# A mixture-of-experts stage on one core: expert blocks of 32 rows on four column groups in place of blocks of 64 on two

## The chip, the cores and the metric

The kernel runs on one core of one Trainium2 chip. The metric is device time in microseconds. TensorE, VectorE (DVE in the rows), ScalarE (ACT), GpSimd (POOL) and SyncE (SP) each run their own stream of instructions and meet at semaphores; transfers run on 16 DMA engines, fed by queues of SyncE, ScalarE and GpSimd.

## The reference, cut to what matters

One step of a decoder layer: a projection, sparse attention and a state-space scan side by side, an output projection, then a mixture of experts and a last norm. 2080 tokens (2048 of the prompt, 32 sampled) each go to 2 of 32 experts. The change concerns the experts:

```python
def run(args):
    xb, e = args                       # rows of one expert, (rows, 1024)
    hdn = jax.nn.silu(xb @ w_gate[e]) * (xb @ w_up[e])      # (rows, 512)
    return hdn @ w_down[e]             # (rows, 1024)
...
contrib = (yr.astype(jnp.float32) * row_w[:, None]).astype(xf.dtype)
return jnp.zeros_like(xf).at[row_tok].add(contrib)
```

All data are float32. One expert's weights are 6 MB: gate and up 1024 x 512 each, down 512 x 1024.

## The kernel before

The program is a row of stages. `mix_out` ends by placing the assignments: each expert's rows are padded to whole blocks of `BR` = 64 slots, every assignment gets a slot, and two one-hot tables (`onerow`, `oneblk`), multiplied on TensorE, give `rows`, the token that stands in each slot of each of up to `MAXBLK` blocks. `experts` works through the blocks in order, and `combine` gathers each token's two result rows from `yslot` in HBM by slot and adds them.

In `experts` every engine walks the same blocks (`over_blocks`): `first` for the first block of an expert, and a loop over `rest` for the others. For block b:

- GpSimd copies the block's token numbers to `cur` and issues two indirect gathers of 128 KB, one for each 32 rows, into `xg` (each token row is spread over four partition groups of 32 as quarters of 256 columns). It starts as soon as VectorE has turned the block before.
- VectorE transposes `xg` into `xT` in squares of 32 (`turn_rows`).
- TensorE (`gate_up`) multiplies `xT`, the stationary operand of 64 columns, with the gate and up weights. The 512 hidden columns are two halves, one on each half of the array's columns, so PSUM partitions 0 to 63 hold the first half for the 64 rows and 64 to 127 the second.
- ScalarE takes Silu of the gate half (`gate`), VectorE multiplies with up (`hidden`), TensorE transposes the product (`turn_hidden`), ScalarE copies it out of PSUM as `hT` (`turned_hidden`).
- TensorE (`down`) multiplies `hT` with the down weights, the 1024 output columns again in two halves. It runs one block late: after the gate/up of block b+1, and it waits for `hT` and for the copy of the block before it out of PSUM.
- VectorE copies the result from PSUM to `y` (`rows_done`). There is one `y`, so the copy of block b waits until all stores of block b-1 have landed (semaphore `y_st`):

```python
def rows_done(b):
    v.wait_ge(sm["y_ok"], 2 * b + 2)
    v.wait_ge(sm["y_st"], 32 * b + 32)
    v.tensor_copy(y[:], py[:]).then_inc(sm["y_cp"], 1)
```

- ScalarE stores `y` to `yslot` in two DMAs of 64 rows by 512 columns (`store`), after the Silu of the next block and before its `turned_hidden`.

SyncE loads the weights of experts into two buffers. The gate and up weights of expert e are issued when the last gate/up of expert e-2 is done, its down weights when the last down of e-2 is done.

Of the kernel before, what the change touches and what calls it, by code (L numbers as in the profile page):

```python
# [15 lines left out]
P = 128  # L16
# [26 lines left out]
BR = 64  # L43
MAXBLK = 98
# [2568 lines left out]
def mix_out(nc, io, keep):  # L2613
# [5 lines left out]
    with Alloc(nc, "mo") as a:  # L2619
# [30 lines left out]
        big = a.sb("big", [P, NT * 2, NEXP])  # L2650
# [5 lines left out]
        oneblk = a.sb("oneblk", [P, NT * 2, MAXBLK])  # L2656
# [121 lines left out]
        def _(v):  # L2778
# [129 lines left out]
            for c in range(2):  # L2908
                sl = slice(q * c, q * c + q)
                v.tensor_tensor(onerow[:, sl, :], bc(rowio[:].unsqueeze(1), [P, q, BR]), bc(lowf[:, sl].unsqueeze(2), [P, q, BR]), ALU.is_equal)  # L2910
                for i in range(q * c, q * c + q):
                    r = slice(0, rows_of(i // 2))
                    v.tensor_scalar(oneblk[r, i, :], blkio[r, :], blkf[r, i:i + 1], keep["tok"][r, i // 2:i // 2 + 1], ALU.is_equal, ALU.mult).then_inc(sm["oh_ok"], 1)
            v.memset(keep["rows"][:, :, MAXBLK:MAXBLK + 1], 0)
            v.wait_ge(sm["map_ok"], 1)
            for q in range(4):
                for hh in range(2):
                    v.tensor_scalar(keep["rows"][32 * q:32 * q + 32, hh, 0:MAXBLK], pl[32 * hh:32 * hh + 32, 0:MAXBLK], 4.0, float(q), ALU.mult, ALU.add)
# [3 lines left out]
        def _(pe):  # L2922
# [51 lines left out]
            for i in range(2 * NT):  # L2974
                r = slice(0, rows_of(i // 2))
                pe.wait_ge(sm["oh_ok"], i + 1)
                mm = pe.matmul(pl[0:BR, 0:MAXBLK], onerow[r, i, :], oneblk[r, i, :], start=(i == 0), stop=(i == 2 * NT - 1))
# [4 lines left out]
def experts(nc, io, keep):  # L2982
# [5 lines left out]
    with Alloc(nc, "ex") as a:  # L2988
# [4 lines left out]
        xg = a.sb("xg", [P, 2, D // 4])  # L2993
        xT = a.sb("xT", [P, KD, 2, 32])
        sg = a.sb("sg", [P, DE // 2])
        hid = a.sb("hid", [P, DE // 2])
        hT = a.sb("hT", [P, 2, 2, BR])
# [3 lines left out]
        names = ("xg_in", "xt_ok", "gu_ok", "sg_ok", "hid_ok", "h_t", "h_ok", "y_ok", "y_cp", "y_st", "zero_ok", "tail_st", "go")  # L3001
        sm = {n: a.sem(n) for n in names}
        gu_in, d_in = [keep["ew_gu_in"], a.sem("gu_in")], [keep["ew_d_in"], a.sem("d_in")]
# [39 lines left out]
        def _(pool):  # L3043
            pool.memset(zero[:], 0.0).then_inc(sm["zero_ok"], 1)
            n = pool.value_load(keep["blocks"][0:1, NEXP:NEXP + 1], min_val=1, max_val=MAXBLK)
            with pool.Fori(0, n + 1) as b:
                pool.wait_ge(sm["xt_ok"], b + 1)
                pool.tensor_copy(cur[:], rows[:, :, ds(b, 1)].squeeze(2))  # L3048
                pool.drain()
                for hh in range(2):  # L3050
                    pool.indirect_dma_start(xg[:, hh, :], None, quarters, bass.IndirectOffsetOnAxis(ap=cur[:, hh:hh + 1], axis=0)).then_inc(sm["xg_in"], 16)  # L3051

        @block.scalar
        def _(s):
# [30 lines left out]
            s.wait_ge(sm["y_st"], n * 32 + 32)  # L3085
# [3 lines left out]
        def _(v):  # L3089
            v.sem_inc(sm["y_cp"], 1)  # L3090
            v.sem_inc(sm["xt_ok"], 1)

            def turn_rows(b):
                v.wait_ge(sm["xg_in"], 32 * b + 32)
# [295 lines left out]
```

## Time and profile before

| | us |
|---|---|
| three runs: median (lowest to highest) | 3298.22 (3292.75 to 3299.91) |
| the profiled execution, its own time | 3290.99 |
| its span, first to last instruction | 3289.2 |
| first gate/up matmul of `experts`, from the span's start | 2276.8 |
| last store of `experts` landed | 3185.8 |

The span is what the profile covers; 1.8 us of the execution's own time lie around it. The stage of the experts is 909 us of it. In the rows below, "idle before" is the time for which an engine waited before an instruction, with what ended it. A matmul of float32 appears as two records.

### The profile page before, as it was taken

The numbers are of one execution on the slowest core, as the hardware profiler recorded it, in microseconds if no ns is written. First come the engines' busy times: TensorE is split into PE (matmuls) and PEld (weight loads), VectorE is DVE, ScalarE is ACT, GpSimd is POOL, SyncE is SP. The second block draws the span as 40 slices with busy tenths as digits, with TensorE's granted clock in tenths as the row PEclk, the third lists the DMA queues.
The fourth block names the chain that finished last, engine by engine and source line by source line (L and its number), as shares of the span: only waits on it lengthen the run. The fifth ranks groups of instructions, "written<-read, shape, count | busy, mean of one in ns | idle before, by whom it ended". The sixth has DMA issues, their size and how long they took to land. (4 is left out here: it accounts for less than half of the span.)

```text
span 3289.2 us, 42132 instructions
## 1 busy us (share of the span) xinstructions
PE 2693.6 (82%) x13682; PEld 1292.4 (39%) x13683; DVE 1626.9 (49%) x3741; ACT 1036.5 (32%) x1887; POOL 815.2 (25%) x940
## 2 busy tenths in 40 slices
PE   7998987966965656777895779995999999999960
PEld 3444333333542334554664544442333333333320
DVE  1146577786766688888873334544111111111126
ACT  1123353573234579874663310010000000000002
POOL 1404031123450333323423400001122121221226
PEclk9999998987877878888997889997999999999985
DMA  6010101012341211100006845543887678787758
GB/s 212 30 49 32 56 13 64 10 37 67 106 131 50 60 31 37 37 27 14 17 14 204 242 124 187 182 133 115 302 299 263 228 259 299 277 288 265 259 186 338
DMA packets 242716, 456.02 MB, mean 139 GB/s; under 512 B 41420, under 2 KB 97214, under 8 KB 242574
## 3 DMA queue, kind: packets, MB, share of 16 engines
q1 hardware_dynamic: 199070, 334.50, 29.7%
q0 software_dynamic: 27872, 89.48, 8.8%
q10 hardware_dynamic: 15632, 30.29, 2.4%
q8 instruction: 71, 1.16, 0.2%
q14 instruction: 71, 0.58, 0.1%
HBM read 368.53 MB, written 85.65 MB: 138 GB/s over the span
## 5 line engine op out<-in xcount | busy, mean ns | idle before, releaser
L784 PE MATMUL pj_cm<-pj_xT,pj_w 128*64 128x512 f32 (+1 forms) x1216 | 397.0, 601 | 8.4 <-ACT pj_xst L682 5.8
L3099 DVE TENSOR_TENSOR ex_hid<-ex_sg,ex_pgu 128x256 f32<-128x256 f32 x83 | 34.9, 421 | 586.5 <-ACT ex_sg L3059 586.5
L3128 PE MATMUL ex_pgu<-pre_down_wgu,ex_xT 128*64 128x512 f32 x1312 | 293.1, 599 | 13.3 <-DVE ex_xT L3095 13.3
L3128 PE MATMUL ex_pgu<-ex_wgu,ex_xT 128*64 128x512 f32 x1344 | 297.7, 595 | 0.4 <-issue 0.4
L784 PEld LDWEIGHTS pj_cm<-pj_xT,pj_w 128*64 128x64 f32 (+1 forms) x1216 | 153.8, 164 | 244.0 <-issue 230.7
L2273 PE MATMUL ap_SB<-keep_kT,ap_qs 64*128 64x512 f32 (+3 forms) x640 | 163.0, 615 | 51.7 <-DVE ap_m L2199 42.5
L2285 PE MATMUL ap_TB<-keep_const,ap_L 128*128 128x128 f32 x1088 | 167.8, 296 | 45.3 <-ACT ap_PT L2021 42.5
L2021 ACT ACTIVATE ap_PT<-ap_TB 128x512 f32<-128x512 f32 (+3 forms) x320 | 154.7, 530 | 150.9 <-PE ap_TB L2285 149.8
L2296 PE MATMUL ap_OB<-ap_PT,keep_V 128*64 128x128 f32 x2176 | 156.4, 305 | 46.6 <-ACT ap_PT L2021 46.6
L3051 POOL DMA_INDIRECT ex_xg<-xn,ex_cur x168 | 161.1, 959 | 104.3 <-issue 104.3
L2285 PEld LDWEIGHTS ap_TB<-keep_const,ap_L 128*128 128x128 f32 x1088 | 124.5, 148 | 149.4 <-issue 63.5
L708 ACT ACTIVATE se_U<-se_sc,se_cand 128x512 bf16<-128x512 f32 (+4 forms) x141 | 162.1, 1151 | 62.9 <-DVEq L529 62.8
L3063 ACT ACTIVATE ex_hT<-ex_ph 128x256 f32<-128x256 f32 x83 | 31.9, 384 | 442.5 <-issue 441.5
L508 DVE TENSOR_SCALAR_CACHE_REDUCE se_U<-se_sc,se_cand 128x384 bf16<-128x384 f32 (+7 forms) x162 | 165.0, 1050 | 12.6
L3048 POOL COPY ex_cur<-pre_rows 128x2 int32 x84 | 15.5, 184 | 617.5 <-DVE ex_xT L3095 617.3
L3128 PEld LDWEIGHTS ex_pgu<-pre_down_wgu,ex_xT 128*64 128x64 f32 x1312 | 91.1, 138 | 186.1 <-issue 172.4
L2031 ACT ACTIVATE ap_L<-ap_L,ap_nm 128x128 f32<-128x128 f32 (+15 forms) x128 | 153.0, 1198 | 35.1 <-DVE ap_nm L2204 30.9
L3128 PEld LDWEIGHTS ex_pgu<-ex_wgu,ex_xT 128*64 128x64 f32 x1344 | 92.9, 137 | 175.3 <-issue 175.3
L2296 PEld LDWEIGHTS ap_OB<-ap_PT,keep_V 128*64 128x64 f32 x2176 | 138.7, 155 | 55.9 <-ACT ap_PT L2021 44.0
L3059 ACT ACTIVATE ex_sg<-ex_pgu 128x256 f32<-128x256 f32 x83 | 31.9, 384 | 401.8 <-PE ex_pgu L3128 401.8
L3144 PE MATMUL ex_py<-ex_wd,ex_hT 128*64 128x512 f32 x672 | 151.4, 592 | 2.3 <-ACT ex_hT L3063 2.3
L2082 DVE TENSOR_SCALAR_CACHE_REDUCE ap_marks<-ap_sc,ap_cand 128x1664 bf16<-128x1664 f32 (+1 forms) x72 | 145.8, 2032 | 5.5
(557 smaller groups left out, 4508.2 us busy)
## 6 DMA issues: line engine op xcount, KB each, us to landing
pre_down_wgu<-in_w_gate SPq DMA_DIRECT2D x16, 2048.0 KB, 9.0
pre_down_wgu<-in_w_up SPq DMA_DIRECT2D x16, 2048.0 KB, 14.8
pre_down_wd<-in_w_down SPq DMA_DIRECT2D x16, 2048.0 KB, 9.4
ex_wgu<-in_w_gate SPq DMA_DIRECT2D x16, 2048.0 KB, 9.3
ex_wgu<-in_w_up SPq DMA_DIRECT2D x16, 2048.0 KB, 14.8
ex_wd<-in_w_down SPq DMA_DIRECT2D x16, 2048.0 KB, 9.6
yslot<-ex_y ACTq DMA_DIRECT2D x166, 128.0 KB, 6.5
pj_x<-in_x_prompt SPq DMA_DIRECT2D x16, 512.0 KB, 4.8
```

Of the source, the lines that this page charges most:

```text
L508: v.tensor_scalar(hits[s][:, 0:keys(h, s)], row_of(h, s), cand[:, s:s + 1].bitcast(F32), None, op, ALU.add, accum_out=cnt[:, s:s + 1])
L708: act_e.activation(hits[s][:, 0:keys(h, s)], row_of(h, s), ACT.Sign, bias=cand[:, s:s + 1].bitcast(F32), scale=-1.0, accum_out=cnt[:, s:s ...
L784: mm = pe.matmul(cm[u % 2][cols * n:cols * n + cols, 0:width_], w[:, k, c0:c0 + cols], xT[:, k, 0:width_], start=(k == 0), stop=(k == KD - 1))
L2021: s_.activation(PT[:, e, o:o + w], TB[t % 2][:, 0:w], ACT.Copy).then_inc(pt_ok, 1)
L2031: s_.activation(L[:, u % 2, e, 0:n], L[:, u % 2, e, 0:n], ACT.Exp, bias=nm[:, h:h + 1], accum_out=rs[:, j % 2, h:h + 1]).then_inc(exp_ok, 1)
L2082: v.tensor_scalar(hits[s][:, 0:keys(s)], row_of(s), cand[:, s:s + 1].bitcast(F32), None, op, ALU.add, accum_out=cnt[:, s:s + 1])
L2273: pe.matmul(SB[:, 2 * (use % 2) + e, 0:w], qs[hs, j % 2, c, :], keep["kT"][hs, o:o + w], start=True, stop=True).then_inc(s_ok, 1)
L2285: mm = pe.transpose(TB[t % 2][:, at:at + P], L[:, u % 2, e, o + at:o + at + P], ident)
L2296: mm = pe.matmul(OB[HD * e:HD * e + HD, P * c:P * c + P], keep["V"][:, kb, HD * e:HD * e + HD], PT[:, e, P * kb:P * kb + P], start=(kb == ...
L3051: pool.indirect_dma_start(xg[:, hh, :], None, quarters, bass.IndirectOffsetOnAxis(ap=cur[:, hh:hh + 1], axis=0)).then_inc(sm["xg_in"], 16)
L3128: mm = pe.matmul(pgu[BR * t:BR * t + BR, :], xT[:, k, :, :], wgu[par][:, k, :, 256 * t:256 * t + 256], start=(k == 0), stop=(k == KD - 1))
L3144: mm = pe.matmul(py[BR * t:BR * t + BR, :], hT[:, k % 2, k // 2, :], wd[par][:, k, 512 * t:512 * t + 512], start=(k == 0), stop=(k == 3))
```

## The change

Blocks become 32 rows long (`BR` = 32, up to 161 of them). A block's columns are spread over four column groups of 32: gate/up takes the 512 hidden columns as four quarters of 128 gate and 128 up columns, down the 1024 output columns as four quarters of 256. The hidden product is then 128 partitions by 128 columns and needs one transpose. The rows of a block come with one gather instead of two; `xg` has two halves, and the gather of block b+2 is issued when the rows of block b have been copied to the new buffer `xa`, from which VectorE transposes. The result is stored by four DMAs of 32 rows by 256 columns. In `mix_out` the one-hot tables take the new sizes (`onerow` 32 columns, `oneblk` 161), and `oneblk` shares its space with an earlier buffer.

```diff
-BR = 64
-MAXBLK = 98
+BR = 32
+MAXBLK = 161
...
-        xg = a.sb("xg", [P, 2, D // 4])
-        xT = a.sb("xT", [P, KD, 2, 32])
+        xg = a.sb("xg", [P, 2 * (D // 4)])
+        xa = a.sb("xa", [P, D // 4])
+        xT = a.sb("xT", [P, KD, BR])
...
-        y = a.sb("y", [P, D // 2])
+        y = a.sb("y", [P, D // 4])
...
-                    sp.wait_ge(sm["gu_ok"], lo * 2)
+                    sp.wait_ge(sm["gu_ok"], lo)
                 load_gate_up(sp, io, wgu[e % 2], e, gu_in[e % 2])
                 if e >= 2:
-                    sp.wait_ge(sm["y_ok"], lo * 2)
+                    sp.wait_ge(sm["y_ok"], lo)
...
-            with pool.Fori(0, n + 1) as b:
-                pool.wait_ge(sm["xt_ok"], b + 1)
-                pool.tensor_copy(cur[:], rows[:, :, ds(b, 1)].squeeze(2))
-                pool.drain()
-                for hh in range(2):
-                    pool.indirect_dma_start(xg[:, hh, :], None, quarters, bass.IndirectOffsetOnAxis(ap=cur[:, hh:hh + 1], axis=0)).then_inc(sm["xg_in"], 16)
+            pool.sem_inc(sm["xg_free"], 2)
+            with pool.Fori(0, (n + 3) >> 1) as g:
+                for half in range(2):
+                    pool.wait_ge(sm["xg_free"], 2 * g + half + 1)
+                    pool.tensor_copy(cur[:, half:half + 1], rows[:, ds(2 * g + half, 1)])
+                    pool.drain()
+                    pool.indirect_dma_start(xg[:, D // 4 * half:D // 4 * half + D // 4], None, quarters,
+                                            bass.IndirectOffsetOnAxis(ap=cur[:, half:half + 1], axis=0)).then_inc(xg_in[half], 16)
...
-                for half in range(2):
-                    s.dma_start(io["yslot"][ds(row, BR), 512 * half:512 * half + 512], y[BR * half:BR * half + BR, :]).then_inc(sm["y_st"], 16)
+                for q in range(4):
+                    s.dma_start(io["yslot"][ds(row, BR), 256 * q:256 * q + 256], y[BR * q:BR * q + BR, :]).then_inc(sm["y_st"], 16)
...
-            def turn_rows(b):
-                v.wait_ge(sm["xg_in"], 32 * b + 32)
-                v.transpose(xT[:].rearrange("p k h t -> p h k t"), xg[:].rearrange("p h (k t) -> p h k t", t=32)).then_inc(sm["xt_ok"], 1)
+            def rows_in(b):
+                v.wait_ge(xg_in[0], 16 * ((b + 2) >> 1))
+                v.wait_ge(xg_in[1], 16 * ((b + 1) >> 1))
+                v.tensor_copy(xa[:], xg[:, ds((b & 1) * (D // 4), D // 4)]).then_inc(sm["xg_free"], 1)
+                v.drain()
+
+            def turn_rows():
+                v.transpose(xT[:], xa[:].rearrange("p (k t) -> p k t", t=32)).then_inc(sm["xt_ok"], 1)
+                v.drain()
...
             def rows_done(b):
-                v.wait_ge(sm["y_ok"], 2 * b + 2)
-                v.wait_ge(sm["y_st"], 32 * b + 32)
-                v.tensor_copy(y[:], py[:]).then_inc(sm["y_cp"], 1)
+                v.wait_ge(sm["y_ok"], b + 1)
+                v.wait_ge(sm["y_st"], 64 * b + 64)
+                v.tensor_copy(y[:], py[:, 0:D // 4]).then_inc(sm["y_cp"], 1)
...
             def rest(b, par):
                 hidden(b)
                 rows_done(b - 1)
+                rows_in(b + 2)
...
                 for k in range(KD):
-                    for t in range(2):
-                        mm = pe.matmul(pgu[BR * t:BR * t + BR, :], xT[:, k, :, :],
-                                       wgu[par][:, k, :, 256 * t:256 * t + 256], start=(k == 0), stop=(k == KD - 1))
+                    for t in range(4):
+                        mm = pe.matmul(pgu[BR * t:BR * t + BR, 0:2 * P], xT[:, k, :],
+                                       wgu[par][:, k, :, P * t:P * t + P], start=(k == 0), stop=(k == KD - 1))
...
                 for k in range(4):
-                    for t in range(2):
-                        mm = pe.matmul(py[BR * t:BR * t + BR, :], hT[:, k % 2, k // 2, :],
-                                       wd[par][:, k, 512 * t:512 * t + 512], start=(k == 0), stop=(k == 3))
+                    for t in range(4):
+                        mm = pe.matmul(py[BR * t:BR * t + BR, 0:D // 4], hT[:, k, :],
+                                       wd[par][:, k, 256 * t:256 * t + 256], start=(k == 0), stop=(k == 3))
```

On ScalarE, in the block loop of an expert, the order before was this (`ex_sg` is the Silu, `ex_hT` the turned hidden rows of the same block, and `yslot<-ex_y` the stores of the block before):

```order
L3059 ACTIVATE ex_sg<-ex_pgu 128x256
L3067 REGISTER_ALU
L3069 ISA
L3069 DMA yslot<-ex_y 64x512
L3069 ISA
L3069 DMA yslot<-ex_y 64x512
L3063 ACTIVATE ex_hT<-ex_ph 128x256
```

And with the change:

```order
L3070 ACTIVATE ex_sg<-ex_pgu 128x128
L3080 ISA
L3080 DMA yslot<-ex_y 32x256
L3080 ISA
L3080 DMA yslot<-ex_y 32x256
L3080 ISA
L3080 DMA yslot<-ex_y 32x256
L3080 ISA
L3080 DMA yslot<-ex_y 32x256
L3074 ACTIVATE ex_hT<-ex_ph 128x128
```

Four issues instead of two now stand between the two activations, each for a quarter of the bytes.

On VectorE, in the same loop, the order before was this (the two `ISA` rows ahead of the copy are its waits for the down projection and for the stores of the block before):

```order
L3099 TENSOR_TENSOR ex_hid<-ex_sg,ex_pgu 128x256
L3094 ISA
L3095 STREAM_TRANSPOSE ex_xT<-ex_xg 128x2x8x32
L3103 ISA
L3104 ISA
L3105 COPY ex_y<-ex_py 128x512
```

And with the change:

```order
L3115 TENSOR_TENSOR ex_hid<-ex_sg,ex_pgu 128x128
L3110 STREAM_TRANSPOSE ex_xT<-ex_xa 128x256
L3120 ISA
L3121 COPY ex_y<-ex_py 128x256
L3104 ISA
L3105 ISA
L3106 REGISTER_ALU x2
L3106 ISA
L3106 COPY ex_xa<-ex_xg 128x256
```

The wait for the gather has moved from ahead of the transpose to behind the copy of `y`, and a copy of the gathered rows is new there.

## Rows read from the trace of the kernel before

**Rows 1.** Windows: the expert stage; busy us and records by engine, granted clock, DMA share.

```profile
core 0: us, PE busy (x) PEld busy (x) DVE busy (x) ACT busy (x) POOL busy (x), PEclk, DMA share, GB/s
...
2276.80:3185.80 909.00, 901.06 (x4150) 296.06 (x4150) 144.34 (x249) 63.76 (x166) 174.45 (x249) 1.00 0.76 264
```

**Rows 2.** Timeline of one block: start, duration, engine, line, what, idle before.

```profile
2601.68 0.69 DVE L3105 COPY ex_y<-ex_py 128x512 f32<-128x512 f32 x1 [2.07 <-PE ex_py L3144]
2601.81 7.09 PE L3128 MATMUL ex_pgu<-pre_down_wgu,ex_xT 128*64 128x512 f32 x32
...
2602.55 1.13 ACTq L3069 DMA_DIRECT2D yslot<-ex_y  x2
2603.73 0.38 ACT L3063 ACTIVATE ex_hT<-ex_ph 128x256 f32<-128x256 f32 x1 [5.20 <-issue]
...
2608.73 3.60 PE L3144 MATMUL ex_py<-ex_wd,ex_hT 128*64 128x512 f32 x16
...
2608.97 0.38 ACT L3059 ACTIVATE ex_sg<-ex_pgu 128x256 f32<-128x256 f32 x1 [4.85 <-PE ex_pgu L3128]
...
2609.73 0.70 DVE L3095 STREAM_TRANSPOSE ex_xT<-ex_xg 128x512 f32<-128x512 f32 x1
...
2610.59 0.18 POOL L3048 COPY ex_cur<-pre_rows 128x2 int32 x1 [7.47 <-DVE ex_xT L3095]
...
2611.71 0.97 POOL L3051 DMA_INDIRECT ex_xg<-xn,ex_cur  x1 [0.94 <-issue]
...
2612.26 0.44 PE L3136 MATMUL ex_ph<-keep_const,ex_hid 128*128 128x128 f32 x2
2612.40 0.37 SPq L196 DMA_DIRECT2D ex_wd<-in_w_down  x1
2612.50 0.69 DVE L3105 COPY ex_y<-ex_py 128x512 f32<-128x512 f32 x1 [2.07 <-PE ex_py L3144]
2612.63 1.08 PE L3128 MATMUL ex_pgu<-pre_down_wgu,ex_xT 128*64 128x512 f32 x4
```

**Rows 3.** The page's groups: one hidden product a block, count, busy, mean ns.

```profile
L3099 DVE TENSOR_TENSOR ex_hid<-ex_sg,ex_pgu 128x256 f32<-128x256 f32 x83 | 34.9, 421 | 586.5 <-ACT ex_sg L3059 586.5
```

**Rows 4.** Timeline of SyncE's weight loads beside three blocks.

```profile
2598.15 0.37 SPq L192 DMA_DIRECT2D ex_wgu<-in_w_gate  x1
2598.56 0.58 SPq L192 DMA_DIRECT2D ex_wgu<-in_w_up  x1
...
2630.61 0.37 SPq L192 DMA_DIRECT2D pre_down_wgu<-in_w_gate  x1
```

**Rows 5.** Line 3069, the two stores at 2602.6 us.

```profile
DMA to landing us min/median/max: 6.2/6.3/6.4
```

**Rows 6.** Line 3069, the two stores at 2613.4 us.

```profile
DMA to landing us min/median/max: 7.2/7.5/7.8
```

**Rows 7.** Line 3069, the two stores at 2624.2 us.

```profile
DMA to landing us min/median/max: 2.6/2.8/2.9
```

**Rows 8.** Timeline of TensorE in the sampled attention: a series on four column groups.

```profile
1790.09 1.95 PE L2602 MATMUL as_OB<-as_V,as_PT 128*32 128x128 f32 x64
```

**Rows 9.** The page's DMA issues: count, KB each, median us from issue to landing.

```profile
ex_wgu<-in_w_gate SPq DMA_DIRECT2D x16, 2048.0 KB, 9.3
ex_wgu<-in_w_up SPq DMA_DIRECT2D x16, 2048.0 KB, 14.8
ex_wd<-in_w_down SPq DMA_DIRECT2D x16, 2048.0 KB, 9.6
```

**Rows 10.** Timeline of VectorE around the start of the expert stage.

```profile
2252.62 1.29 DVE L2910 TENSOR_TENSOR mo_onerow<-mo_rowio,mo_lowf 128x1088 f32<-128x1088 f32 x1
2253.83 4.17 DVE L2913 TENSOR_SCALAR mo_oneblk<-mo_blkio,mo_blkf,keep_const 128x98 f32<-128x98 f32 x17
...
2276.08 0.71 DVE L3095 STREAM_TRANSPOSE ex_xT<-ex_xg 128x512 f32<-128x512 f32 x1 [10.20 <-DMA ex_xg<-xn,ex_cur]
```

**Rows 11.** Windows: a stretch with a recurring gap on TensorE.

```profile
990.00:1050.00 60.00, 40.75 (x219) 17.03 (x217) 39.91 (x58) 35.09 (x43) 0.32 (x1) 0.86 0.08 30
```

**Rows 12.** Timeline of TensorE in that stretch: the gap and its period.

```profile
1004.33 2.81 PE L1719 MATMUL ss_X<-ss_sw,ss_shw 128*128 128x512 f32 x4 [2.58 <-ACT ss_sw L1584]
...
1013.95 1.98 PE L1719 MATMUL ss_X<-ss_sw,ss_shw 128*128 128x512 f32 x4 [2.58 <-ACT ss_sw L1584]
```

More of the change, by code:

```diff
@@ L2655, in mix_out, with oneblk @@
         blki, blkf = a.sb("blki", [P, NT * 2], I32), a.sb("blkf", [P, NT * 2])
-        oneblk = a.sb("oneblk", [P, NT * 2, MAXBLK])
+        ownblk = a.sb("ownblk", [P, OWN, MAXBLK])
+        def oneblk(r, i):
+            return ownblk[r, i, :] if i < OWN else spare[r, (i - OWN) * MAXBLK:(i - OWN + 1) * MAXBLK]
         tp = a.ps("tp")
@@ L2976, in _ @@
                 pe.wait_ge(sm["oh_ok"], i + 1)
-                mm = pe.matmul(pl[0:BR, 0:MAXBLK], onerow[r, i, :], oneblk[r, i, :], start=(i == 0), stop=(i == 2 * NT - 1))
+                mm = pe.matmul(pl[0:BR, 0:MAXBLK], onerow[r, i, :], oneblk(r, i), start=(i == 0), stop=(i == 2 * NT - 1))
             mm.then_inc(sm["map_ok"], 1)
@@ L2992, in experts @@
         cur = a.sb("cur", [P, 2], I32)
[L2993 to L2998 removed]
+        xg = a.sb("xg", [P, 2 * (D // 4)])
+        xa = a.sb("xa", [P, D // 4])
+        xT = a.sb("xT", [P, KD, BR])
+        sg = a.sb("sg", [P, P])
+        hid = a.sb("hid", [P, P])
+        hT = a.sb("hT", [P, 4, BR])
+        y = a.sb("y", [P, D // 4])
         zero = a.sb("zero", [BR, D])
         pgu, ph, py = a.ps("pgu"), a.ps("ph"), a.ps("py")
[L3001 removed]
+        names = ("xg_free", "xt_ok", "gu_ok", "sg_ok", "hid_ok", "h_t", "h_ok", "y_ok", "y_cp", "y_st", "zero_ok", "tail_st", "go")
         sm = {n: a.sem(n) for n in names}
+        xg_in = [a.sem(f"xg_in{i}") for i in range(2)]
         gu_in, d_in = [keep["ew_gu_in"], a.sem("gu_in")], [keep["ew_d_in"], a.sem("d_in")]
@@ L3114, in rest @@
                 rows_done(b - 1)
-            turn_rows(0)
+                rows_in(b + 2)
+            v.wait_ge(xg_in[0], 16)
+            v.tensor_copy(xa[:], xg[:, 0:D // 4]).then_inc(sm["xg_free"], 1)
+            v.drain()
+            turn_rows()
+            v.wait_ge(xg_in[1], 16)
+            v.tensor_copy(xa[:], xg[:, D // 4:D // 2]).then_inc(sm["xg_free"], 1)
+            v.drain()
             over_blocks(v, first, rest)
@@ L3124, in gate_up @@
             def gate_up(b, par):
-                pe.wait_ge(sm["xt_ok"], b + 2)
+                pe.wait_ge(sm["xt_ok"], b + 1)
                 for k in range(KD):
-                    for t in range(2):
-                        mm = pe.matmul(pgu[BR * t:BR * t + BR, :], xT[:, k, :, :],
-                                       wgu[par][:, k, :, 256 * t:256 * t + 256], start=(k == 0), stop=(k == KD - 1))
-                        if k == KD - 1:
-                            mm.then_inc(sm["gu_ok"], 1)
+                    for t in range(4):
+                        mm = pe.matmul(pgu[BR * t:BR * t + BR, 0:2 * P], xT[:, k, :],
+                                       wgu[par][:, k, :, P * t:P * t + P], start=(k == 0), stop=(k == KD - 1))
+                mm.then_inc(sm["gu_ok"], 1)
             def turn_hidden(b):
                 pe.wait_ge(sm["hid_ok"], b + 1)
-                for k in range(2):
-                    mm = pe.transpose(ph[:, k * P:(k + 1) * P], hid[:, k * P:(k + 1) * P], ident)
-                mm.then_inc(sm["h_t"], 1)
+                pe.transpose(ph[:, 0:P], hid[:], ident).then_inc(sm["h_t"], 1)
             def down(b, par):
@@ L3354, in trunk_step @@
         with Alloc(nc, "pre") as b:
-            keep["rows"] = b.sb("rows", [P, 2, MAXBLK + 1], I32)
+            keep["rows"] = b.sb("rows", [P, MAXBLK + 3], I32)
             keep["wo"], keep["wo_in"] = b.sb("wo", [P, KD, D]), b.sem("wo_in")
```

35 lines of the change are left out of this document (18 added, 17 removed).

## The prediction

> **What bounds the kernel now.** I began with the windows of the expert stage. From the first gate/up matmul (2276.8 us) to the landing of the last store (3185.8 us) TensorE is busy 901 of 909 us, its granted clock is 1.00, and the DMA engines are busy 0.76 of the time [rows 1]. So in this stage TensorE is the limit and everything else has room. The timeline of one block then shows the rhythm [rows 2]: gate/up starts at 2601.81 and again at 2612.63, so a block of 64 rows costs 10.82 us. Gate/up takes 6.92 us to the start of the down projection, down 3.53 us to the two transposes of the hidden rows, these 0.37 us. The page counts 83 blocks [rows 3]: 83 x 10.82 = 898 us.
>
> In the same timeline the reader should see a loop that does not touch TensorE. VectorE copies the finished rows out of PSUM into the one buffer `y` (0.69 us), 0.18 us later ScalarE issues two stores (1.13 us), and the next copy into `y` waits until both have landed. How long landing takes depends on what SyncE has in flight. The store at 2602.6 has the next expert's gate and up weights (issued 2598.15) beside it and lands after 6.2 and 6.4 us; the one at 2613.4 has the down weights beside it: 7.2 and 7.8 us; the one at 2624.2 has none: 2.6 and 2.9 us [rows 4 to 7]. The second of two stores is issued 0.64 us after the first (1.13 less its own 0.49). At its worst the loop is 0.69 + 0.18 + 0.64 + 7.8 = 9.3 us. That is under 10.82, so today it costs nothing: VectorE's copy is always released by TensorE [rows 2].
>
> **The change, part by part.**
>
> *Padding and TensorE.* Counting the routing of the reference's inputs gives 4160 row assignments, 81 to 174 an expert: 83 blocks of 64, as the page has it, and 147 of 32. Each 32-row block streams half the columns (256 for 512) through four column groups instead of two. If a group of four costs what a pair does per column, gate/up and down take (6.92 + 3.53) / 2 = 5.23 us. That four groups of 32 do run side by side is shown elsewhere in the trace: 64 matmul records of 128 columns in 1.95 us, 0.122 us a group of four [rows 8]; at 256 columns and 24 groups that bounds the block from above at 24 x 0.244 = 5.86 us (the series' start and end are in it). I take 5.23, because the matmuls of the experts are the same stream. One transpose instead of two: 0.2 to 0.37, taken as 0.30. Block: 5.53 us. 147 x 5.53 = 813 us, **85 us less** (between 85 less and 7 more at 5.86 + 0.30).
>
> *VectorE, ScalarE and the gather.* A 256-column operation with PSUM input takes 0.42 us where 512 columns take 0.69 [rows 2, 3]. VectorE has per block: hidden product, transpose, copy of `y`, and the new copy of the gathered rows, each at most 0.42: under 1.7 of 5.53 us. ScalarE's two activations shrink from 0.38 each. POOL needs 2.1 us from its release to the end of an indirect DMA's issue (2610.59 to 2612.68 [rows 2]), and now has one a block and two blocks, 11 us, for it to land. The stage's first pair of gathers, beside weights and with POOL's start-up, is in after 10.2 us of VectorE's waiting [rows 10], so one gather has more time than two took there; I cost this edit at nothing. If that cover failed, VectorE would wait in the row copy, and the next hidden product behind it.
>
> *Four stores instead of two, and one `y`.* This is the part that decides. ScalarE issues four in 3 x 0.64 + 0.49 = 2.4 us, ahead of the copy of the turned hidden rows, for which the next down projection waits. Without any wait for landings that chain is: end of down to copy 0.17 (2612.33 to 2612.50), copy 0.42, 0.18, issues 2.4, turned hidden rows some 0.38 (between half and all of today's 0.38, with 0.05 of signalling on each side), down 1.8 us (half of 3.60): 5.3 us, just under 5.53. So the issues are hidden, barely. The landing is not. The copy of block b still waits for all stores of b-1, and the loop is 0.42 + 0.18 + 0.05 + L, where L runs from the first issue to the last landing. It exceeds 5.53 when L is over 4.88 us. With no weights in flight the last of four is issued 1.92 us after the first and takes 2.6 to 2.9: L = 4.8 at most; the loop stays hidden. With weights in flight there are three bounds from [rows 5, 6]: the whole set lands with the first store, 6.2 (gate/up) and 7.2 (down); as the present pair, 0.64 + 6.4 = 7.0 and 8.4; each small store needs the whole latency from its own issue, 1.92 + 6.4 = 8.3 and 9.7. In the present pair the second needs as long from its own issue as the first, so I take a value between the second and third bounds, **7.7 and 9.0 us**. The block then lasts 8.35 us beside gate/up and 9.65 beside down.
>
> How long are weights in flight? Gate and up are issued 0.41 us apart and land 14.8 us after the second issue: 15.2 us [rows 4, 9]. Down, issued before that end, follows with half their bytes: 7 us (today 8.6, since it is issued only 1 us before the others land). Per load 15.2 / 8.35 + 7 / 9.65 = 2.55 blocks take 22.2 us in place of 14.1: 8.1 us more. Loads for experts 2 to 31 run beside blocks: 30 x 8.1 = **243 us more**. Queued behind VectorE's wait are its row copy, which frees the gather buffer, and the next hidden product; ScalarE's stores and turned hidden rows wait for the copy, and TensorE's next down projection for those.
>
> *Placement tables.* The one-hot rows go from 98 to 161 columns, 34 of them at 0.245 us [rows 10], at most 0.16 us more each, and the other table halves (two of 1.29). Between 1 us less and 5 more; taken as 0. The zero fill of unused slots runs behind the last weights on SyncE, ahead of the stage's end.
>
> Sum: -85 + 243 = +158 us. The profiled execution took 3290.99 us (span 3289.2), so 3449; it lies 7 us under the median of the three runs shown, so I say **3450**. With the lowest L (6.2, 7.2) the blocks last 6.85 and 7.85 us, a load costs 5.0 us extra, and the sum is +65: 3356. With the highest it is 9.1 us, +187: 3478.
>
> **Where a page disagrees.** No row shows a 32 KB store; the 128 KB stores range from 2.6 us alone to 7.8 beside weights [rows 5 to 7]. The Trainium skill, page "DMA: Bandwidth & Descriptors", section "Anatomy of one DMA", gives a fitted 2.0 us plus bytes at 436 GB/s for a DMA (fitted for those GpSimd issues), so 2.1 us for 32 KB; by it L would be 4.0 us, the loop would stay hidden, and the sum would be -85. The trace agrees with it only where no weights move. The same page's rules for kernel authors advise against many transfers under 64 KB.
>
> **The rivals.**
> - *The stores land in time; TensorE sets the pace; faster.* Small stores of half the bytes might slip between weight packets. It decides if L is under 4.88 us beside weights. For it: 2.6 to 2.9 us alone, half the bytes, and a longer period leaves the DMA engines idler. Against: over half of the present latency beside weights is not there without them (6.4 to 7.8 against 2.9), and that part need not shrink with the bytes. 3291 - 85 = 3206 us, with the median's offset 3210. Chance 0.15. The rule of the Trainium skill's page "DMA: Bandwidth & Descriptors" named above would end here.
> - *The clock falls too.* Beside weights TensorE now has one gap of 2.8 to 4 us a block. Gaps of 2.58 us every 9.6 us stand earlier in the trace, and there the mean granted clock is 0.86 of full speed, switching between 2.4 and 1.2 GHz [rows 11, 12]. Inside a waiting block slower matmuls fit into the gap; but if after each load half of a gate/up (1.7 us) still runs at the lower level, that costs 1.7 us a load: +51 us, 3500. Chance 0.12.
> - *The column groups don't overlap.* Then 24 groups cost twice as much, 10.76 us a block: 147 x 10.76 - 898 = +684, 3975. [Rows 8] speak against it. Chance 0.02.
> - *Gain and loss cancel* (L near 5.7, 2.8 us a load): chance 0.05.
>
> **How the numbers follow.** My case has 0.66 with its own range of 3356 to 3500. The likeliest is 3450; the range of 3300 to 3540 leaves out the faster rival and the last one. Faster 0.15, same 0.05, slower 0.80; 0.2% (6.6 us) is about what a measurement of this kernel can tell.
>
> **What would show it.** Right: VectorE's copy of `y` waits for the DMA of `y` to the slots in 2 to 3 blocks of each expert, block periods are of two kinds (about 5.5, and 8 to 10 us), TensorE idles some 200 us in the stage waiting for the turned hidden rows, and the stage lasts near 1065 us. Each step is wrong if: blocks without weights last longer than 5.7 us (TensorE's size or the issue chain); VectorE is still released by TensorE everywhere (the loop); row copies wait for the gather (the cover); loads take other than 22 us. The prediction falls if the last of four stores lands within 5 us beside weights.

## The result, and the profile after

The changed kernel takes 3320.5 us (median of 7 runs, 3310.25 to 3325.21), the kernel before 3292.75 us beside it: a ratio of 1.0081 (95% interval 1.0066 to 1.0097), **0.8% slower**, some 28 us. The forecast was 3450. The profiled execution took 3324.2 us, 33.2 more than the one shown before.

The window of the expert stage, from the first gate/up matmul to the landing of the last store (columns as in [rows 1]):

```profile
core 0: us, PE busy (x) PEld busy (x) DVE busy (x) ACT busy (x) POOL busy (x), PEclk, DMA share, GB/s
2275.28:3218.66 943.38, 847.25 (x14259) 465.30 (x14259) 200.50 (x589) 80.32 (x294) 171.93 (x297) 0.98 0.69 247
```

Against [rows 1] TensorE is busy 54 us less, and idle 96 us where it was 8: 88 more. The difference, 34 us, is all by which the two profiled executions differ (33.2). The waits of that stage say for what TensorE idles, and who else waits (us in total, times, longest):

```profile
DVE ex_y L3121 <- DMA yslot<-ex_y: 182.1, 69, 5.9
DVE ex_y L3121 <- PE ex_py L3165: 84.9, 78, 3.9
PE ex_py L3165 <- ACT ex_hT L3074: 64.4, 46, 6.1
PE ex_pgu L3152 <- issue: 25.3, 31, 1.1
```

Before, TensorE released VectorE's copy into `y` in all 83 blocks:

```profile
DVE ex_y L3105 <- PE ex_py L3144: 174.3, 83, 5.6
```

Now the copy waits for the landing of stores in 69 of 147 blocks. TensorE's down projection waits 64 us for the turned hidden rows. The last row was not in the forecast: at each of 31 changes of expert TensorE waits up to 1.1 us for its own sequencer. The timeline of one load shows how these hang together (gate and up issued at 2653.2, down at 2661.6):

```profile
2653.16 0.37 SPq L192 DMA_DIRECT2D pre_down_wgu<-in_w_gate  x1
...
2655.01 0.42 DVE L3121 COPY ex_y<-ex_py 128x256 f32<-128x256 f32 x1 [0.89 <-PE ex_py L3165]
2655.61 1.85 ACTq L3080 DMA_DIRECT2D yslot<-ex_y  x4
2656.15 3.66 PE L3152 MATMUL ex_pgu<-ex_wgu,ex_xT 128*32 128x256 f32 x64 [1.07 <-issue]
...
2661.59 0.37 SPq L196 DMA_DIRECT2D pre_down_wd<-in_w_down  x1
2661.73 3.66 PE L3152 MATMUL ex_pgu<-ex_wgu,ex_xT 128*32 128x256 f32 x64
2662.10 0.42 DVE L3121 COPY ex_y<-ex_py 128x256 f32<-128x256 f32 x1 [1.27 <-DMA yslot<-ex_y]
2662.70 1.78 ACTq L3080 DMA_DIRECT2D yslot<-ex_y  x4
...
2667.30 3.66 PE L3152 MATMUL ex_pgu<-ex_wgu,ex_xT 128*32 128x256 f32 x64
2669.30 0.42 DVE L3121 COPY ex_y<-ex_py 128x256 f32<-128x256 f32 x1 [2.89 <-DMA yslot<-ex_y]
2669.91 1.76 ACTq L3080 DMA_DIRECT2D yslot<-ex_y  x4
2671.73 0.28 ACT L3074 ACTIVATE ex_hT<-ex_ph 128x128 f32<-128x128 f32 x1 [5.99 <-issue]
2672.05 1.93 PE L3165 MATMUL ex_py<-ex_wd,ex_hT 128*32 128x256 f32 x32 [1.09 <-ACT ex_hT L3074]
2674.17 0.43 DVE L3121 COPY ex_y<-ex_py 128x256 f32<-128x256 f32 x1 [1.17 <-PE ex_py L3165]
```

An undisturbed block lasts 5.57 to 5.58 us (gate/up at 2661.73 and at 2667.30). From copy to copy the store loop takes 7.09 us, then 7.20, then 4.87: two long turns in this load, 3.1 us over two blocks. TensorE loses only the 1.07 us of the expert's change and 1.3 us before the last down projection: 1.09 us of standing still, and the 0.2 us by which an undisturbed down projection's records begin ahead of the end of gate/up's. The other 0.8 us is room that the chain has.

The trace also records every raising of the semaphore `y_st`, 16 for each store. For the four stores issued from 2662.70 on, 0.48 us apart, these come in four groups of 16 that end at 2667.42, 2667.97, 2668.52 and 2669.28. So the set doesn't land at one moment: taken in order, each store lands 4.7 to 5.1 us after its own issue. In the 65 sets that land late (over 4.5 us after the first issue, of 94 sets that the trace records whole) the medians for the four are 4.8, 5.0, 5.0 and 5.2 us. The two stores of 128 KB before took 6.7 and 7.5 us, counted the same way over 62 late sets.

### The profile page after: what moved, and what is told of

Same layout as the page of the kernel before. It is cut to its first block and busy times, and to the rows that moved or that the text cites. A ratio compares the mean times of both kernels' runs of the same rounds, so it can differ in the third digit from the quotient of the medians.

```text
span 3322.4 us, 65872 instructions
## 1 busy us (share of the span) xinstructions
PE 2634.5 (79%) x23791; PEld 1449.3 (44%) x23792; DVE 1682.5 (51%) x4078; ACT 1052.6 (32%) x2015; POOL 810.1 (24%) x988
## 5 line engine op out<-in xcount | busy, mean ns | idle before, releaser
L3152 PE MATMUL ex_pgu<-pre_down_wgu,ex_xT 128*32 128x256 f32 x4800 | 279.2, 385 | 20.6 <-DVE ex_xT L3110 12.1
L3152 PE MATMUL ex_pgu<-ex_wgu,ex_xT 128*32 128x256 f32 x4608 | 263.6, 380 | 16.9 <-issue 16.9
L3074 ACT ACTIVATE ex_hT<-ex_ph 128x128 f32<-128x128 f32 x147 | 40.8, 278 | 726.4 <-issue 724.0
L3115 DVE TENSOR_TENSOR ex_hid<-ex_sg,ex_pgu 128x128 f32<-128x128 f32 x147 | 42.3, 288 | 445.4 <-ACT ex_sg L3070 443.7
L3152 PEld LDWEIGHTS ex_pgu<-pre_down_wgu,ex_xT 128*32 128x32 f32 x4800 | 150.4, 111 | 124.2 <-issue 17.1
L3121 DVE COPY ex_y<-ex_py 128x256 f32<-128x256 f32 x147 | 62.4, 425 | 267.0 <-DMA yslot<-ex_y 182.1
L3152 PEld LDWEIGHTS ex_pgu<-ex_wgu,ex_xT 128*32 128x32 f32 x4608 | 143.6, 110 | 112.1 <-issue 20.1
L3057 POOL COPY ex_cur<-pre_rows 128x1 int32 x150 | 27.5, 183 | 628.1 <-DVE ex_xa L3106 627.8
L3165 PE MATMUL ex_py<-pre_down_wd,ex_hT 128*32 128x256 f32 x2400 | 147.0, 386 | 32.4 <-ACT ex_hT L3074 32.0
L3165 PE MATMUL ex_py<-ex_wd,ex_hT 128*32 128x256 f32 x2304 | 143.9, 392 | 32.4 <-ACT ex_hT L3074 32.3
```

The lines of the kernel that those rows point to most:

```text
L3121: v.tensor_copy(y[:], py[:, 0:D // 4]).then_inc(sm["y_cp"], 1)
L3152: mm = pe.matmul(pgu[BR * t:BR * t + BR, 0:2 * P], xT[:, k, :], wgu[par][:, k, :, P * t:P * t + P], start=(k == 0), stop=(k == KD - 1))
L3165: mm = pe.matmul(py[BR * t:BR * t + BR, 0:D // 4], hT[:, k, :], wd[par][:, k, 256 * t:256 * t + 256], start=(k == 0), stop=(k == 3))
```

## The experiments

Each is the changed kernel with the edit shown.

**The turned hidden rows ahead of the stores** (e1_hidden_first).

```diff
     gate(b)
-    store(b - 1)
     turned_hidden(b)
+    store(b - 1)
```

> The changed kernel with one edit on ScalarE: the turned hidden rows are copied ahead of the four stores instead of behind them; still one y. Theory A (the landing loop reaches TensorE only through the chain copy of y, four issues, turned hidden rows, down projection, which has little slack): TensorE's waits for the turned hidden rows, 64 us in the profile of the changed kernel, nearly vanish, while VectorE's copy still waits for the landing in two blocks of each load; 3255 us (3245 to 3270). Theory B (as predicted: the loop of copy, issue and landing is itself the pace beside weights, wherever ScalarE puts the issues): the down projection waits for the copy instead; at most 20 us better, 3300 or more. Theory C (the loss is TensorE's own: expert boundaries and clock): no change, 3320.

Measured: 3285.7 us, 0.9983 of before (0.9968 to 0.9998). Theory C falls. The waits of its stage:

```profile
DVE ex_y L3121 <- DMA yslot<-ex_y: 199.7, 90, 5.9
PE ex_ph L3158 <- DVE ex_hid L3115: 25.9, 27, 5.5
PE ex_py L3165 <- DVE ex_y L3121: 3.6, 4, 1.3
```

The copy waits as before for the landing, and the 64 us for the turned hidden rows are gone from TensorE's waits. So ScalarE's order decides how much of the landing TensorE feels. But a new wait has come: when the copy is late, the four issues run past the end of gate/up, the Silu stands behind them, and TensorE waits 26 us for the hidden product. This is most of the 31 us by which the run lies above theory A's number.

**Two halves of `y`, one semaphore** (e2_two_halves), in the order of e1_hidden_first.

```diff
+    s.wait_ge(sm["y_st"], 64 * b + 128)      # stores of b-1 landed
     s.wait_ge(sm["y_cp"], b + 2)
...
-    v.tensor_copy(y[:], py[:, 0:D // 4]).then_inc(sm["y_cp"], 1)
+    v.tensor_copy(y[:, ds((b & 1) * (D // 4), D // 4)], py[:, 0:D // 4]).then_inc(sm["y_cp"], 1)
```

> As e1_hidden_first, and y has two halves: the copy of a block waits for the stores of two blocks ago, and ScalarE waits for the landing of one set of stores before it issues the next. Theory A: the copy's waits for the stores go to about zero, but hardly anything was left on TensorE's path, so within 10 us of e1_hidden_first, about 3250. Theory B: the landing loop falls from L + 0.65 us to L (6.0 to 6.8 us) and clearly beats e1_hidden_first by 30 us or more. Theory C: no change, 3320.

Measured: 3311.9 us, ratio 1.0060 (1.0039 to 1.0080): 26 us above e1_hidden_first, which no theory had.

```profile
ACT ex_sg L3070 <- DMA yslot<-ex_y: 156.1, 28, 10.9
PE ex_ph L3160 <- DVE ex_hid L3117: 47.5, 33, 6.4
```

The edit only moved the wait: ScalarE now stands in it, ahead of the next Silu, and TensorE waits 48 us for the hidden product. It says nothing on what two halves are worth.

**One store in place of four** (e3_one_store).

```diff
-    for q in range(4):
-        s.dma_start(io["yslot"][ds(row, BR), 256 * q:256 * q + 256], y[BR * q:BR * q + BR, :]).then_inc(sm["y_st"], 16)
+    s.dma_start(io["yslot"][ds(row, BR), :].rearrange("r (q c) -> q r c", q=4), y[:]).then_inc(sm["y_st"], 16)
```

> The changed kernel with the four stores of a block replaced by one DMA of the same 128 KB; order and y as in the changed kernel. If each small store needs the whole latency from its own issue (the upper bound of the prediction), the set lands 1.44 us earlier beside weights (4.6 to 5.4 us after the first issue in place of 6.0 to 6.8). If the set lands together, when the weight packets ahead of it are through (the lowest bound), landing stays at 6.0 to 6.8 us after the issue and only the 1.3 us of issues ahead of the turned hidden rows go. By theory A both give 3255 to 3275 us, and the landing time tells them apart; by theory B the second gives no more than 15 us; by theory C no change, 3320.

Measured: 3455.9 us, ratio 1.0507 (1.0485 to 1.0528). Neither landing time came. Copies and issues beside one load:

```profile
2489.58 0.56 ACTq L3079 DMA_DIRECT2D yslot<-ex_y  x1
...
2499.05 0.43 DVE L3120 COPY ex_y<-ex_py 128x256 f32<-128x256 f32 x1 [4.24 <-DMA yslot<-ex_y]
2499.65 1.05 ACTq L3079 DMA_DIRECT2D yslot<-ex_y  x1
...
2509.47 0.42 DVE L3120 COPY ex_y<-ex_py 128x256 f32<-128x256 f32 x1 [7.60 <-DMA yslot<-ex_y]
```

From issue to waiting copy 9.5 and 9.8 us, against 6.5 and 6.6 in the changed kernel. The DMA view of that first set counts 132 packets, and 192 in the changed kernel, for the same 128 rows of 1 KB: 4 more than the rows, against 64. At no time are more than 4 of its packets in flight, against 10 of the changed kernel's set, and at the landing it raises the semaphore 4 times (2498.73 to 2499.02), against 64. That fits 4 engines at work on this one DMA, and 16 on each of the four small ones. As a test of the two bounds the run fails; as a test of the loop it serves: landings 3 us longer cost 135 us. Its stage, and TensorE's wait in it:

```profile
2276.18:3348.00 1071.82, 888.08 (x14259) 474.30 (x14259) 200.64 (x589) 78.60 (x294) 172.16 (x297) 0.94 0.60 217
```

```profile
PE ex_py L3164 <- ACT ex_hT L3074: 153.0, 61, 4.4
```

TensorE waits 89 us more for the turned hidden rows, and it is busy 41 us more, at a granted clock of 0.94 for 0.98.

**No weight loads** for experts 2 to 31 (e4_no_weights).

```diff
-    load_gate_up(sp, io, wgu[e % 2], e, gu_in[e % 2])
+    sp.sem_inc(gu_in[e % 2], 32)          # from expert 2 on; load_down likewise
```

> The changed kernel without the weight loads of experts 2 to 31 (they compute with the weights of experts 0 and 1), every wait kept by counting the semaphores up. Theory A and B: no copy of y waits for stores, no wait of TensorE for the turned hidden rows, every block inside an expert 5.58 us; what is left of the stage over 147 x 5.58 = 820 us is the expert boundaries (25 us of TensorE waiting for its own sequencer) and the end: 3245 us (3235 to 3255). Theory C: the time is that of the changed kernel within 10 us.

Measured (one run): 3244.9 us. Its stage, and its waits:

```profile
2278.17:3140.34 862.17, 827.59 (x14259) 468.67 (x14259) 200.73 (x589) 81.36 (x294) 171.56 (x297) 0.99 0.18 51
```

```profile
PE ex_pgu L3155 <- issue: 25.8, 31, 1.1
PE ex_py L3168 <- ACT ex_hT L3077: 2.9, 2, 2.7
```

Weights beside the blocks cost 79 us between the two profiled executions (76 from the changed kernel's median): TensorE's waits for the turned hidden rows go from 64 to 3, and it is busy 20 us less, at a granted clock of 0.99 for 0.98. The changes of expert keep their 25 us.

**Queues exchanged** (e6_queues_swapped): SyncE stores, ScalarE loads the weights, zero fill of unused slots first.

```diff
     gate(b)
-    store(b - 1)
     turned_hidden(b)
+    load(b, par, j)          # in an expert's first block; the stores are SyncE's
```

> The changed kernel with the two users of queues exchanged: SyncE walks the blocks and issues the four stores, ScalarE issues an expert's three weight loads behind the turned hidden rows of the next expert's first block; the zero fill of unused slots goes ahead of the first block. One y, the copy still waits for the landing. Theory (the landing loop costs TensorE only what ScalarE's issues hang on to it, ahead of the turned hidden rows in the changed kernel, ahead of the Silu in e1_hidden_first): waits for the turned hidden rows and for the hidden product both go to a few us, though the copy of y waits for the stores as long as before (180 to 200 us); left are the expert boundaries (25 to 28 us) and the start: 3245 us (3235 to 3260). Rival (the landing itself, through the copy that the down projection waits for, is the pace beside weights): the waits move to the copy and the time stays at e1_hidden_first's 3286 or above. Against the theory too: weights are issued some 5 us later, and if an expert of three blocks waits for them, 3260 to 3280.

Measured: 3337.5 us, ratio 1.0147 (1.0132 to 1.0161). The theory isn't tested, since two costs of the edit's own cover it:

```profile
2648.22 4.44 ACTq L3083 DMA_DIRECT2D ex_wd<-in_w_down  x1
2652.85 0.28 ACT L3087 ACTIVATE ex_sg<-ex_pgu 128x128 f32<-128x128 f32 x1 [5.64 <-PE ex_py L3174]
```

```profile
PE ex_ph L3167 <- DVE ex_hid L3124: 41.9, 27, 2.5
PE ex_py L3174 <- DVE ex_y L3130: 35.5, 11, 27.7
```

The third load, right behind two others, occupies ScalarE 4.4 us (0.37 on SyncE, 8 us later), and the Silu waits behind it: 42 us. And one wait of 27.7 us: SyncE's count-up of the semaphore for 147 used blocks, which belongs to the zero fill, lay ahead of the first stores. Between its last zero fill (ends at 2275.6) and its first store (2322.8) SyncE issues nothing; the 147 counts of the semaphore stand in the trace from 2275.8 to 2321.0, 45 us.

**A bound carried in a register** (e7_bounds_carried).

```diff
-    lo = eng.value_load(keep["blocks"][0:1, ds(e, 1)], ...)
+    lo = hi of the expert before, in every second expert
```

> The changed kernel with one edit: in every second expert the first block's number is not loaded from SBUF again but taken from the register that ended the expert before; on TensorE's sequencer one load and its checks (0.71 us) less at 15 of 31 boundaries. Theory (TensorE idles at a boundary because its sequencer loads two bounds one after the other, 1.5 us): the 15 gaps of 0.6 us go, 9 us, 3311 (3307 to 3315), and the other 16 of 1.1 us stay. Rival (the gap is the jump or the wait for the weights): no change, 3320.

Measured: 3316.1 us, ratio 1.0089 (1.0075 to 1.0103); the changed kernel had 1.0081. No gain.

```profile
PE ex_py L3167 <- ACT ex_hT L3076: 73.6, 50, 6.1
PE ex_pgu L3154 <- issue: 16.9, 16, 1.1
```

The gaps are the loads, as the theory said: 15 of 31 vanish, 8.4 us. But the waits for the turned hidden rows grow by 9.2. It seems that the gap had only given the store loop time that TensorE lost anyway; the last kernel below bears on that.

**Zero fill early** (e5_zero_early). SyncE's zero fill beside the last loads makes a set of stores expensive in the changed kernel:

```profile
3157.86 6.43 ACTq L3080 DMA_DIRECT2D yslot<-ex_y  x4
3164.33 0.28 ACT L3074 ACTIVATE ex_hT<-ex_ph 128x128 f32<-128x128 f32 x1 [11.45 <-issue]
3164.66 3.64 PE L3165 MATMUL ex_py<-pre_down_wd,ex_hT 128*32 128x256 f32 x32 [6.12 <-ACT ex_hT L3074]
```

```diff
     load_down(sp, io, wd[e % 2], e, d_in[e % 2])
+    if e == 1: zero fill of the unused slots and its count-up, which stood behind the loop
```

> The changed kernel with one edit on SyncE: the zero fill of the unused slots (14 DMAs of 128 KB) is issued behind the weights of expert 1 instead of behind those of the last expert. Theory (the zero fill beside the last loads holds ScalarE's store issues for 6.4 us and makes one block 13.8 us long): the long block goes, 8 to 11 us, 3311. Rival: the same collision takes place with the first blocks' stores or gathers instead, 3320.

Measured: 3326.8 us, ratio 1.0113 (1.0098 to 1.0128). TensorE's waits for the turned hidden rows fall to 54.7 us, but the count-up, moved along, holds the loads of expert 2, and TensorE waits for them once:

```profile
PE ex_pgu L3153 <- DMA pre_down_wgu<-in_w_up: 18.6, 1, 18.6
```

The late set is explained by the fill; the gain from moving it wasn't obtained.

**The gather one block later** (e8_gather_later).

```diff
-    pool.sem_inc(sm["xg_free"], 2)
+    pool.sem_inc(sm["xg_free"], 1)
```

> The changed kernel with one edit on GpSimd: a gather is released one block later (one free half at the start instead of two), so each has one block and not two to land. If the second block of lead is what makes the gather free, VectorE's copy of the gathered rows waits beside weights by 2 to 3 us a block (2.1 us to the end of the issue and about 6 to land against 5.6) and the kernel loses 10 us or more; if one block is enough, no wait shows in the copy and the time stays at 3320.

Measured (one run): 3315.8 us, within the changed kernel's runs. VectorE's copy of the gathered rows does wait, in 94 blocks, two thirds of them beside weights:

```profile
DVE ex_xa L3106 <- DMA ex_xg<-xn,ex_cur: 124.0, 94, 6.5
PE ex_ph L3158 <- DVE ex_hid L3115: 11.1, 8, 3.1
```

TensorE pays 11 us for it, and its waits for the turned hidden rows are 13 us fewer. So the second block of lead hides a wait (2.3 us in one place is left with it), but here that is worth nothing that one run can tell, perhaps because the same blocks are late for `y` already.

**Two stores of 64 KB** (e12_two_stores).

```diff
-    for q in range(4):
-        s.dma_start(io["yslot"][ds(row, BR), 256 * q:256 * q + 256], y[BR * q:BR * q + BR, :]).then_inc(sm["y_st"], 16)
+    for q in (0, 2):
+        s.dma_start(io["yslot"][ds(row, BR), 256 * q:256 * q + 512].rearrange("r (i c) -> r i c", i=2),
+                    y[BR * q:BR * q + BR, :].unsqueeze(1).to_broadcast([BR, 2, 256])).then_inc(sm["y_st"], 16)
```

> The changed kernel with two stores of 64 KB a block instead of four of 32 KB: the same number of 1 KB rows and bytes, but the first and third quarter of the result are written twice (into their own place and the next one), so the second and fourth are left out of the output. Which of the prediction's bounds for the landing holds. If each store needs its own time from its own issue (in the changed kernel the last of four is issued 1.44 us after the first and lands 4.6 to 5.3 us later), the last of two, issued 0.48 us after the first, lands 5.1 to 5.8 us after it beside weights, and with 0.96 us less of issues ahead of the turned hidden rows TensorE's waits for these fall from 64 us to under 15: 3255 to 3270. If the set lands together, once the weight packets ahead are through, landing stays at 6.0 to 6.8 us, only the issues get shorter, and the time is 3280 to 3300.

Measured (one run): 3256.0 us, before 3288.1 beside it. The landing and the time part ways:

```profile
2400.08 0.92 ACTq L3080 DMA_DIRECT2D yslot<-ex_y  x2
2406.30 0.42 DVE L3122 COPY ex_y<-ex_py 128x256 f32<-128x256 f32 x1 [1.20 <-DMA yslot<-ex_y]
2406.90 0.81 ACTq L3080 DMA_DIRECT2D yslot<-ex_y  x2
2413.38 0.42 DVE L3122 COPY ex_y<-ex_py 128x256 f32<-128x256 f32 x1 [2.70 <-DMA yslot<-ex_y]
```

```profile
PE ex_py L3166 <- ACT ex_hT L3074: 10.5, 12, 2.4
```

From first issue to waiting copy 6.2 and 6.5 us, against 6.5 and 6.6 with four. That doesn't show that a set lands together, for each store now carries twice the bytes: by the semaphore's raisings the two land 5.2 and 5.7 us after their own issues (medians of 72 late sets), where those of 32 KB take 4.8 to 5.2. Fewer issues and longer landings about cancel. Yet TensorE's waits fall from 64 us to 10, since the issues ahead of the turned hidden rows are 0.9 us shorter.

**Two halves of `y`, a semaphore for each.** Three kernels: the changed order, the hidden rows first, and this with the carried bound.

```diff
-    for q in range(4): ... y[BR * q:BR * q + BR, :] ... .then_inc(sm["y_st"], 16)
+    for half in range(2):
+        with s.If(s.snap((b + 1 + half) & 1)):
+            for q in range(4): ... y[BR * q:BR * q + BR, 256 * half:256 * half + 256] ... .then_inc(y_st[half], 16)
...
-    v.wait_ge(sm["y_st"], 64 * b + 64)
+    v.wait_ge(y_st[0], 64 * ((b + 2) >> 1) + 64)      # stores up to b-2 landed
+    v.wait_ge(y_st[1], 64 * ((b + 3) >> 1) + 64)
```

> The changed kernel with two halves of y and a semaphore for each (a branch on ScalarE picks the half), so the copy of a block waits for the stores of two blocks ago and nothing waits for the landing of the block before; the four issues stay ahead of the turned hidden rows. Theory (all that the weights cost TensorE, 79 us between the changed kernel and e4_no_weights, comes through the one y, as waits, as the clock after long waits, and beside the zero fill): VectorE's copy waits for no store, TensorE's waits for the turned hidden rows fall from 64 us to under 10, no or few stretches at the lower clock; e4's 3245 us plus some 5 to 10 for the zero fill beside the last loads: 3252 (3243 to 3265). Rival (ScalarE's issues, slower beside weights, are themselves late, whatever y does): the waits for the turned hidden rows stay at 40 us or more and the time at 3290 or above. Second rival: the branch costs ScalarE more than the 0.25 us of room in its chain, and every block becomes longer than 5.58 us.

> As e9_two_y, with the turned hidden rows copied ahead of the four stores. Theory: with the copy of y on time the issues fit between the turned hidden rows and the next Silu, so TensorE's waits for the hidden product (26 us in e1_hidden_first) go too; within 8 us of e9_two_y, about 3250, and it doesn't depend on the branch's price. Rival (the stores keep the Silu late even so): 3270 or more.

> As e10_two_y_hidden_first, with the bound of a block carried in a register as in e7_bounds_carried. In e7 the 8.4 us less of boundary gaps came back as 9 us more of waiting for the turned hidden rows. Theory (a boundary's gap gave the landing loop time, and with two halves nothing takes it back): 8 us (5 to 10) below e10_two_y_hidden_first, about 3242. Rival (the boundaries lie where TensorE would wait anyway): no difference.

Measured: **3259.3** us (ratio 0.9901, 0.9884 to 0.9917), **3251.3** (0.9884, 0.9869 to 0.9899) and **3235.1** (0.9835, 0.9820 to 0.9851). In the first, the copy starts at the same distance behind its down projection whether weights are in flight or not, 0.6 to 0.7 us in 146 of 147 blocks:

```profile
2663.65 1.93 PE L3171 MATMUL ex_py<-pre_down_wd,ex_hT 128*32 128x256 f32 x32
2665.78 3.66 PE L3158 MATMUL ex_pgu<-pre_down_wgu,ex_xT 128*32 128x256 f32 x64
2666.22 0.42 DVE L3127 COPY ex_y<-ex_py 128x256 f32 x1 [1.41 <-DMA yslot<-ex_y]
...
2671.46 0.85 PE L3158 MATMUL ex_pgu<-pre_down_wgu,ex_xT 128*32 128x256 f32 x12
```

0.64 us after the end of the matmuls (2665.58), so the DMA named in the bracket had long been done. TensorE's waits for the turned hidden rows fall to 9.4 us. The second rival is right in small: registers and branch use up the chain's room, and this block lasts 5.68 us. With the hidden rows first that goes too. The waits of the last kernel:

```profile
PE ex_pgu L3160 <- issue: 16.7, 16, 1.3
PE ex_ph L3166 <- DVE ex_hid L3122: 6.8, 4, 3.6
```

With `y` out of the way the carried bound is worth what its gaps are (25.6 to 16.7 us): the same edit gave nothing in e7_bounds_carried. The medians differ by 16 us, the two profiled executions by 12, and from the stage's first matmul to its last by 9.0 (862.3 and 853.3 us); the rest lies outside the stage.

## Why the prediction was right in direction and wrong in size

*TensorE's block: right.* 5.58 us measured for 5.53, so 147 blocks (hidden products on the page, below) x 5.58 = 820 us, 78 below 898 where 85 was forecast. Four column groups run side by side.

```profile
L3115 DVE TENSOR_TENSOR ex_hid<-ex_sg,ex_pgu 128x128 f32<-128x128 f32 x147 | 42.3, 288 | 445.4 <-ACT ex_sg L3070 443.7
```

*The store loop on one `y`: the mechanism right, the term of 243 us mis-sized.* Of its signs the waits are there: the copy waits for the DMA of `y`, 69 times in 30 loads, and TensorE idles for the turned hidden rows. The blocks of 8 to 10 us aren't: 7 of the 146 periods from gate/up to gate/up are over 8 us, and the stage lasts 943 us and not 1065. The loop cost 64 us of idle. A load is in flight for 20.3 us (median), 22.2 in the forecast. Two steps failed.

The first is "I take a value between the second and third bounds, 7.7 and 9.0 us". From the first issue to the waiting copy it is 6.5 and 6.6 us. That is near the first bound (6.2, 7.2), but not for its reason, since the set doesn't land with the first store. The third bound had the form right: every store has a latency of its own, and the last is issued last. What was too large is that latency, taken as the 6.4 us and more of stores with four times the bytes; a 32 KB store takes 4.8 to 5.2 us beside weights. The issues are also closer, 0.48 us apart and not 0.64 (1.76 us for four, not 2.4). So L is 1.45 + 5.2 = 6.65 us by the medians. The turns are 7.1, 7.2 and 4.9 us and not 8.35 and 9.65.

The second is that each turn's length was taken as the block's. A block becomes longer only by the lateness that is left when the room of the chain is used up, and this room, set by what ScalarE does ahead of the turned hidden rows, was forecast as 0.2 us. It was 0.8 us, and of 3.1 us of lateness in the load shown TensorE stood still for 1.09 before a down projection. Moving ScalarE's issues (e1_hidden_first) or shortening them (e12_two_stores) took nearly all of these waits away with the landing as it was. With landings of 9.5 and 9.8 us (e3_one_store) the time is 3456 us. That this is close to the forecast is chance: the forecast had shorter turns, no room to speak of, and no clock.

*Not in the forecast: the change of expert.* 25 us of TensorE's waits for its sequencer, where [rows 1] leave 8 us of idle in all. e4_no_weights has them without weights, e7_bounds_carried shows that they are the loading of the bounds.

*The clock.* The rival's mechanism is real but small. After the long waits TensorE runs for a while at the lower of its two levels (1.2 GHz): 3.17 us of matmul in 3.5 us at a granted 0.51, while the down projections of other blocks take 1.9.

```profile
2320.70:2324.20 3.50, 3.17 (x32) 1.38 (x32) 0.64 (x2) 0.55 (x2) 0.50 (x1) 0.51 0.23 62
```

It follows 2.6 us of waiting for the turned hidden rows; 6 of the 147 down projections take 3.2 to 3.6 us. It goes with the waits: e4_no_weights is busy 20 us less. Summed by tile, TensorE is busy 290.9 us in the down projections, 542.8 in gate/up and 49.2 in the hidden products, there 282.2, 541.7 and 48.4. So the slower matmuls cost 10.5 us; the rival had 51. The rest of the 20 fits the 0.2 us of overlapping records that each of the 46 waits takes away (9 us, an estimate).

The sum, from measured terms: -78 + 64 + 25 + 20 = +31 us; the profiled executions differ by 33. The direction was right by luck, then. The forecast's own two terms come out at -78 and +64, and with all that the weights cost (79 us by e4_no_weights) gain and loss cancel; what made the kernel slower is the change of expert, which the forecast didn't have. In time the rival "gain and loss cancel" came nearest, though not by its L near 5.7 us.

*The placement tables, at nothing: right.* The stage begins at 2275.3 us, before at 2276.8, and after its last store's landing 104 us are left, before 103.

*The gather, at nothing: right.* VectorE waits 2.3 us in one place for it.

*The rival that stores land in time: wrong beside weights.* Its rule, of the Trainium skill's page "DMA: Bandwidth & Descriptors", section "Anatomy of one DMA" (2.0 us plus the bytes at 436 GB/s, fitted for DMAs that GpSimd issues), gives an estimate of 2.3 us for 128 KB. The zero fill's DMAs, which SyncE issues, have that size: in e4_no_weights they land in 2.1 us (median of 14), in the changed kernel, beside loads, in 8.4. So the trace agrees with the rule without weights and not beside them. The rival's own condition, L under 4.88 us, isn't met either: L is 6.5.

## What to carry to other kernels

When a buffer's reuse waits for a landing, don't multiply the loop's length by the blocks it meets: add up how late it gets in one burst of traffic, subtract the room of the chain behind it, and charge the limiting engine the rest. Take the landing time from DMAs of the same size under the same traffic. First look at what an in-order engine issues ahead of the work that feeds that engine; putting it behind, or giving each half of the buffer its own semaphore, turned 0.8% slower into 1.2% faster here (both together). A gap that you remove while another loop is the limit comes back as that loop's wait; try it again when the loop is gone.

## What the runs showed of the hardware that was not expected

- Beside weight loads, a store on ScalarE's queue landed 4.8 to 5.2 us after its own issue with 32 KB, 5.2 to 5.7 with 64 KB (e12_two_stores) and 6.7 to 7.5 with 128 KB (before); stores issued 0.48 us apart landed one after the other.
- One store of 128 KB with four quarters as its outermost dimension never had more than 4 packets in flight and landed 3 us later beside weights (9.5 and 9.8 us) than four of 32 KB (6.5 and 6.6).
- A third load of 2 MB, issued right behind two others from ScalarE, took 4.44 us to issue in e6_queues_swapped; from SyncE, also right behind two others, it took 4.24 us in e5_zero_early, and 8 us later it takes 0.37.
- A loop that counts up a semaphore for 147 blocks kept SyncE for 45 us (e6_queues_swapped).
- TensorE waits up to 1.1 us for its sequencer at each of 31 changes of expert, where two bounds are loaded from SBUF, and before it waited so once, for 0.4 us. Per microsecond there are some three times as many matmul records as before (14259 in 943 us, 4150 in 909); that this is the reason wasn't tested.
